# The samples' outer product in HGRN2 and retention heads: on VectorE with values broadcast by DMA, in place of row-tiled matmuls on TensorE

## The chip, the cores and the metric

The kernel runs on one core of a Trainium2 chip. The metric is the device time of one execution in microseconds. The profile is of one more execution of the same program, taken by the hardware profiler; all times inside it are counted from the start of its span.

## What is computed

Two decoder layers run on a prompt of 512 tokens and on 8 samples of one token each, which share the weights. Every layer has 16 heads of width 128: 4 of the HGRN2 kind, 6 of the mLSTM kind and 6 of the retention kind. Each sample brings a state of 128x128 for every head, takes one step and gives the new state back. For one token the HGRN2 and retention steps come to the same form: the state is scaled (by row in HGRN2, by one number in retention), the outer product of the token's key and value is added, and the query reads the result:

```
s_new = decay * s + k[:, None] * v[None, :]     # 8 samples, each head, 128 x 128
o     = q @ s_new
```

The reference has it as chunked scans whose chunk is one token long for the samples:

```python
s_new = (jnp.exp(b_last[:, :, 0, :])[..., None] * s
         + jnp.einsum('bhsk,bhsv->bhkv', kc * jnp.exp(b_last - b), vc))        # HGRN2
...
s_new = (chunk_d[None, :, None, None] * s
         + jnp.einsum('bhsk,bhsv->bhkv', kc * state_d[None, :, :, None], vc))  # retention
```

## The kernel before

**Tiles.** Activations lie transposed, features on partitions, with the 512 prompt tokens and the 8 sample tokens side by side as 520 columns (`TOK`; `T` is 512, `NS` is 8). A product of 128 output features with all tokens is one *tile*: 16 blocks of 128 inputs, each as three matmuls of 260 columns for two halves of the tokens (`quarter`), 96 matmuls in all, accumulated in the PSUM tensor `pj`. Weights come from HBM as 1 MB loads into `raw`; ScalarE makes their rounded part `whi`, GpSimd the rest `wlo`.

**Heads.** A head has four tiles, numbered 0 to 3: two for query and key (or the gate), one for v, one for the output gate z. The order of heads in a layer is one retention head, four HGRN2 heads, six mLSTM heads, five retention heads (`KINDS`). Head h of layer l has the number g = 16 l + h; n counts heads of one kind.

**The order of the work.** Each engine runs its own program in order, and the programs meet in semaphores. TensorE runs tile after tile. A tile is cut into eight *parts* of 12 matmuls, and between parts the small products of the heads are called (`hooks_of`): for retention and mLSTM heads `scores` and `rows` after part 1 of tile 3, `states_u` after part 4, `outputs` after part 7 (the tile's end); HGRN2 heads have `rows` after part 2, `states_u` after part 4, `outputs` after part 7. Layer 0's first head has `states_u` and `outputs` after parts 2 and 4 of the next head's tile 0. The z tile of the head is tile 3, the one in which all this stands.

**The samples' step in a plain head** (HGRN2 or retention) of before:
- ScalarE copies v (columns of all tokens) out of PSUM (`take(2, v, 0)`), then rounds the weights of a later tile (`high`), then copies the sample columns of q, k and v into `apart`, two to each group of 32 columns (`rows`, `by_four`).
- TensorE transposes v and k in chunks (`v_rows`, `k_rows`) and the three parts of `apart` (`sample_rows`), all into the PSUM tensor `mx`.
- ScalarE copies the samples' rows to `sr`, v's rows to `vt` and k's rows to `kt`. `vt` lies over the buffer `v`.
- VectorE spreads the samples' v over `big` in a block pattern (`blocks`), scales the state `ss` by the decay, and waits for `states_u`.
- TensorE, in `states_u`, forms the prompt's state increments from `kt` and `vt` (four products of 128x128), and in four row groups of two rows the samples' outer products from `sr` and `big` into columns 256 to 511 of `mx`.
- VectorE runs the chain of prompt states over four chunks into `st`, then adds the samples' products to `ss`. `outputs` on TensorE reads `st` and `ss`.

SyncE issues all DMAs of before in program order: weight loads (`load(t, par, src)`, which waits for the semaphore `lo_done` of the tile two before), the store of the last head's new states, the fetch of the next head's states (which waits until every earlier store has landed), and for mLSTM heads three rows broadcast from HBM. `big` is part of `lev`, a buffer that HGRN2 heads use for their levels.

## Time and profile before

| | us |
|---|---|
| median of 3 runs (2323.57 to 2324.18) | 2323.64 |
| profiled execution: its own time | 2323.17 |
| profiled execution: its span | 2321.6 |

| engine | busy us | share of the span |
|---|---|---|
| TensorE (matmul) | 2266.9 | 98% |
| VectorE | 1283.8 | 55% |
| GpSimd | 907.0 | 39% |
| ScalarE | 738.1 | 32% |

How to read the rows further down: PE is TensorE's matmul stream, PEld its weight loads, DVE is VectorE, ACT ScalarE, POOL GpSimd, SP or SPq SyncE's queue. L1046 is line 1046 of the kernel before. Matmuls overlap in the array, so the duration of one is longer than its distance from the next. A plain fp32 matmul is recorded as two. The profiler's timeline merges neighbours of one line and operands into one row with a count; its duration runs from the first start to the last end.

### The profile page before, as it was taken

How to read it: one execution, taken by the hardware profiler on the slowest of the kernel's cores; microseconds unless marked ns; L12 is line 12 of the kernel's file. 1: busy time of each engine (PE TensorE's matmuls, PEld its weight loads, DVE VectorE, ACT ScalarE, POOL GpSimd, SP SyncE). 2: the span in 40 equal slices, each digit the busy share in tenths (PEclk: the TensorE clock that was granted, in tenths of full speed). 3: DMA queues.
4: the chain of work that ended last, by engine and by line, in shares of the span. 5: the costliest groups of instructions: out<-in, count | busy, mean ns of one | idle time of the engine just before them, and what ended most of it. 6: DMA issues, size and time to landing. Idle time of an engine off the chain costs nothing.

```text
span 2321.6 us, 50275 instructions
## 1 busy us (share of the span) xinstructions
PE 2266.9 (98%) x21347; PEld 2161.7 (93%) x21347; DVE 1283.8 (55%) x2506; ACT 738.1 (32%) x1175; POOL 907.0 (39%) x668
## 2 busy tenths in 40 slices
PE   4899999999999999999999999999999999999998
PEld 3799999999999999998879999999999999999998
DVE  6346666677776344442126566567777753435444
ACT  2143322333333333421124333233333433334111
POOL 3033333333334343554333333333333443346542
PEclk9999999999999999999999999999999999999999
DMA  9952222554453333366775222244453333323332
GB/s 400 378 185 93 93 94 97 162 164 160 159 178 99 116 99 117 103 219 239 267 268 201 77 93 93 91 161 156 166 164 107 112 101 124 113 86 109 121 112 106
DMA packets 153647, 347.21 MB, mean 150 GB/s; under 512 B 14816, under 2 KB 85408, under 8 KB 127544
## 3 DMA queue, kind: packets, MB, share of 16 engines
q1 hardware_dynamic: 153424, 344.01, 43.1%
q8 instruction: 168, 2.75, 0.5%
q14 instruction: 55, 0.45, 0.1%
HBM read 312.07 MB, written 32.09 MB: 148 GB/s over the span
## 4 chain that ended last, share of the span: by engine, by line
PE 89%; DVE 4%; DMA 2%; DVEq 1%; POOL 1%; ACT 1%; issue 1%; SPq 0%; ACTq 0%; POOLq 0%
PE pj L685 72%; PE mx L691 3%; PE mx L1028 2%; DMA rows<-in_ada_first 1%; PE mx L1054 1%; PE mx L1042 1%; PE mx L778 1%; PE mx L744 1%; POOL wlo L653 1%; DMA spare_piece<-in_ada_first 1%; DVE t L1501 1%; PE pj L1150 1%; PE mx L1006 1%; PE mx L1056 1%; PE mx L1046 1%; PE mx L937 1%
## 5 line engine op out<-in xcount | busy, mean ns | idle before, releaser
L685 PE MATMUL pj<-hh,whi 128*128 128x260 f32 x4928 | 1418.0, 288 | 4.7 <-DVE hl L1501 3.2
L685 PE MATMUL pj<-hl,whi 128*128 128x260 f32 x4928 | 1392.8, 283 | 0.0
L685 PE MATMUL pj<-hh,wlo 128*128 128x260 f32 x4928 | 1390.6, 282 | 0.0
L653 POOL TENSOR_TENSOR wlo<-raw,whi 128x512 fp32r<-128x512 f32 x632 | 862.6, 1395 | 1323.5 <-ACT whi L1229 1323.5
L685 PEld LDWEIGHTS pj<-hh,whi 128*128 128x128 f32 x4928 | 928.1, 188 | 52.5 <-issue 46.2
L685 PEld LDWEIGHTS pj<-hl,whi 128*128 128x128 f32 x4928 | 928.5, 188 | 0.0
L685 PEld LDWEIGHTS pj<-hh,wlo 128*128 128x128 f32 x4928 | 928.0, 188 | 0.0
L1229 ACT ACTIVATE whi<-raw 128x2048 fp32r<-128x2048 f32 x158 | 302.9, 1917 | 256.8 <-PE pj L685 186.8
L1229 ACT ACTIVATE xv<-pj 128x260 f32<-128x260 f32 x188 | 64.7, 383 | 380.2 <-PE pj L685 379.9
L1501 DVE SCALAR_TENSOR_TENSOR o<-pj,mod,t 128x260 f32<-128x260 f32 (+1 forms) x56 | 24.6, 480 | 230.1 <-PE pj L685 214.5
L1229 ACT ACTIVATE t<-t 128x520 f32<-128x520 f32 (+1 forms) x126 | 79.2, 629 | 182.1 <-DVEq L1761 132.8
L1501 DVE SCALAR_TENSOR_TENSOR t<-xv,prm_bia,t 128x512 f32<-128x512 f32 x96 | 100.3, 1065 | 5.5
L1229 ACT ACTIVATE z<-pj 128x260 f32<-128x260 f32 x64 | 21.3, 385 | 242.0 <-PE pj L685 240.1
L1495 DVE TENSOR_TENSOR xv<-xv,lev 128x520 f32<-128x520 f32 x24 | 19.7, 819 | 121.7 <-ACT t L1229 121.2
L1495 DVE TENSOR_TENSOR t<-mx,hc 128x512 f32<-128x512 f32 x12 | 8.3, 692 | 112.0 <-PE mx L1006 112.0
L1229 ACT ACTIVATE zw<-zw 128x520 f32<-128x520 f32 x96 | 61.4, 639 | 25.0 <-DVEq L1734 20.7
L1495 DVE TENSOR_TENSOR zw<-zw,z 128x520 f32<-128x520 f32 x42 | 55.7, 1327 | 3.1
L724 PE MATMUL mx<-rows,sct 128*32 128x128 f32 x704 | 26.9, 302 | 30.7 <-DMA rows<-in_ada_first 30.6
L1495 DVE TENSOR_TENSOR lev<-sr,cst 98x256 f32<-98x256 f32 x44 | 36.8, 836 | 33.6 <-ACT sr L1229 33.6
L724 PEld LDWEIGHTS mx<-rows,sct 128*32 128x32 f32 x704 | 20.7, 121 | 35.2 <-issue 22.7
L691 PE MATMUL mx<-cst,xv 128*128 128x128 f32 x352 | 49.1, 273 | 1.6 <-DVEq L1991 1.5
L1951 DVE COPY xv<-mx 128x512 f32<-128x512 f32 x20 | 13.9, 693 | 65.4 <-PE mx L1065 65.4
(290 smaller groups left out, 2283.3 us busy)
## 6 DMA issues: line engine op xcount, KB each, us to landing
raw<-in_w_tiles SPq DMA_DIRECT2D x128, 1024.0 KB, 4.9
raw<-in_wo_tiles SPq DMA_DIRECT2D x32, 1024.0 KB, 5.0
lev<-in_w_ada SPq DMA_DIRECT2D x90, 256.0 KB, 4.6
rows<-in_ada_first SPq DMA_DIRECT2D x22, 1024.0 KB, 21.1
lev<-in_w_ada SPq DMA_DIRECT2D x39, 512.0 KB, 5.7
out<-ss SPq DMA_DIRECT2D x32, 512.0 KB
xv<-in_w_ada SPq DMA_DIRECT2D x25, 512.0 KB, 5.8
y_kept<-o SPq DMA_DIRECT2D x2, 4160.0 KB, 17.9
```

The lines of the kernel that those rows point to most:

```text
L653: last = e.tensor_tensor((wlo_third if t == 2 else wlo[:, par, :])[:, cs], w[:, cs], high_of(t)[:, cs].bitcast(F32), ALU.subtract)
L685: last = e.matmul(pj[:, 2 * par + b, 0:HALF], w[:, par, kb * P:(kb + 1) * P], x[:, kb, b * HALF:(b + 1) * HALF], start=(kb == 0 and m == 0 ...
L691: return e.transpose(out, src, cst[0:n, C_ID:C_ID + n])
L724: last = e.matmul(mx[32 * j:32 * j + 32, 2 + which, 0:n], sct[:, FIRST_K * i + x, :], w[:, j], start=(i == 0 and x == 0), stop=(p == piece ...
L744: last = e.matmul(mx[32 * j:32 * j + 32, 3, x * P:(x + 1) * P], sct[:, SESSION_K * (session % 4) + i, :], at[:, j * P:(j + 1) * P], start= ...
L778: last = e.matmul(mx[r:r + 32, n % 2, :], sct[:, kb, :], ada_slot(piece)[:, j, :], start=(kb < 4), stop=(kb >= KB - 4))
L937: last = e.matmul(mx[32 * j:32 * j + 2 * H_ML, 0, 0:QUART], gw[:, kb, :], x[:, kb, j * QUART:(j + 1) * QUART].bitcast(F32), start=(kb == 0 ...
L1006: last = e.matmul(mx[:, 0, c * CH:(c + 1) * CH], k[:, c * CH:(c + 1) * CH], q[:, c * CH:(c + 1) * CH], start=True, stop=True)
L1028: last = e.matmul(mx[64 * b:64 * b + 64, bank, 64 * c:64 * c + 64], key[:, s0:s0 + 64], query, start=True, stop=True)
L1229: return e.activation(out, in_, func, **kw)
L1495: return e.tensor_tensor(out, a_, b_, op)
L1501: return e.scalar_tensor_tensor(out=out, in0=a_, scalar=s, in1=b_, op0=op0, op1=op1)
```

## The change

The change applies to the HGRN2 and retention heads; mLSTM heads keep their way.

- After the copy of v, ScalarE issues a DMA that stores the samples' columns of v (128 partitions x 8) into a DRAM tensor `v_kept` of 8 rows of 128 floats (`keep_v`). The store's pieces are single floats.
- SyncE waits for that store, for the previous head to be done and for the head's last score products, and then issues a DMA that reads `v_kept` (4 KB) into `big` on each of the 128 partitions. It stands ahead of the load of the weight tile `t + 5`.
- TensorE's `sample_rows` and the products with `big` are only issued for mLSTM heads. `states_u` of retention heads (but layer 0's first) moves from part 4 to part 3 of tile 3.
- ScalarE drops the copies of `apart` and `sr` in plain heads, and waits for the store to have landed before it writes `vt`, which lies over v.
- VectorE drops `blocks` and the addition from PSUM in plain heads. The new `outer` multiplies `big` by the key columns and adds the product to `ss`: ahead of the chain of prompt states in HGRN2 heads, behind it in retention heads.

```diff
...
+        v_kept = nc.dram_tensor("v_kept", [NS, HD], F32, kind="Internal").ap()
...
+        v_saved, v_in = sem("v_saved"), sem("v_in")
...
+        def plain_before(g):
+
+            return sum(KINDS[x % NH] != "ml" for x in range(g))
...
                     for j in range(2):
                         if (l, h, j) == (0, 0, 0):
                             continue
+                        if j == 1 and kind != "ml":
+                            e.wait_ge(v_saved, 16 * (plain_before(g) + 1))
+                            e.wait_ge(head_done, g + 1)
+                            e.wait_ge(ps["score"], scorec(l, h, LEVELS + 1 if kind == "hg" else 1))
+                            e.dma_start(big, v_kept.rearrange("s d -> (s d)").partition_broadcast(P)).then_inc(v_in, 16)
...
                             v_rows()
-                            k_rows()
-                            sample_rows().then_inc(ps["tr"], 1)
+                            last = k_rows()
+                            if kind == "ml":
+                                last = sample_rows()
+                            last.then_inc(ps["tr"], 1)
...
                             e.wait_ge(vs["a"], g + 1)
-                            e.wait_ge(vs["blk"], g + 1)
                             e.wait_ge(as_["vt"], g + 1)
                             e.wait_ge(as_["kt"], g + 1)
-                            e.wait_ge(as_["sr"], g + 1)
+                            if kind == "ml":
+                                e.wait_ge(vs["blk"], n + 1)
+                                e.wait_ge(as_["sr"], n + 1)
                             w = HD + 1 if kind == "ml" else HD
                             for c in range(NC):
                                 last = e.matmul(mx[:, c, 0:w], kt[:, c, :], vt[:, c, 0:w], start=True, stop=True)
-                            lhs = sw if kind == "ml" else sr[:, 1, :]
-                            for j in range(4):
-                                r = slice(32 * j, 32 * j + 2)
-                                last = e.matmul(mx[:, j, 256:512], lhs[r, :], big[r, 0:256], start=True, stop=True)
+                            if kind == "ml":
+                                for j in range(4):
+                                    r = slice(32 * j, 32 * j + 2)
+                                    last = e.matmul(mx[:, j, 256:512], sw[r, :], big[r, 0:256], start=True, stop=True)
...
-                        return ({}, {}, {1: (scores, rows), 4: (states_u,), 7: (outputs,)}), {5: (back,)}
+                        return ({}, {}, {1: (scores, rows), 3: (states_u,), 7: (outputs,)}), {5: (back,)}
...
                             last.then_inc(taken, 1)
+                            if kept is not None:
+                                kept()
...
                         def rows(scaled):
...
+                            e.wait_ge(ps["tr"], g + 1)
+                            if scaled == "ml":
+                                act(sr[0:GR], mx[0:GR, 3, 0:3 * HD].rearrange("p (j d) -> p j d", j=3), ACT.Copy).then_inc(as_["sr"], 1)
                             else:
...
+                                e.wait_ge(v_saved, 16 * (plain_before(g) + 1))
                             act(vt[:, :, 0:HD], mx[:, 1, :].rearrange("p (c d) -> p c d", c=NC), ACT.Copy).then_inc(as_["vt"], 1)
...
+                        def keep_v():
+
+                            e.wait_ge(taken, ht(g, 2))
+                            e.wait_ge(v_in, 16 * plain_before(g))
+                            e.dma_start(v_kept.rearrange("s d -> d s"), v[:, T:TOK],
+                                        allow_slow_non_contiguous=True).then_inc(v_saved, 16)
...
-                            take(2, v, 0)
+                            take(2, v, 0, kept=keep_v)
...
-                        else:
-                            blocks(sr[0:GR, 2, :], big[0:GR, 0:256])
-                        e.drain().then_inc(vs["blk"], 1)
+                            e.drain().then_inc(vs["blk"], 1)
...
+                        def outer():
+
+                            e.wait_ge(v_in, 16 * (plain_before(g) + 1))
+                            vb = big.rearrange("p (s d) -> p s d", s=NS)
+                            tt(vb, vb, bc(k[:, T:TOK], 2, HD), M)
+                            e.drain()
+                            tt(ss, ss, vb, A_)
+                            e.drain()
+
+                        if kind == "hg":
+                            outer()
                         e.wait_ge(ps["u"], g + 1)
...
-                        tt(ss4, ss4, mx[:, 0:4, 256:512], A_)
+                        if kind == "ml":
+                            tt(ss4, ss4, mx[:, 0:4, 256:512], A_)
+                        elif kind == "rt":
+                            outer()
                         e.drain().then_inc(vs["ss"], 1)
```

What stands in a row on the engines is shown at three places. Line numbers are those of each kernel; the words in brackets are the semaphores that an instruction waits for.

ScalarE, retention head 12 of layer 0, from the copy of v to the copy of z; `xv` holds the buffers of v and `vt`, `t` that of `kt`. Before:

```order
L1229 ACTIVATE xv<-pj 128x260 [waits tile_done]
L1229 ACTIVATE xv<-pj 128x260
L1229 ACTIVATE whi<-raw 128x2048 [waits tile_done,raw_in0]
L1229 ACTIVATE apart<-xv 128x12x2 [waits taken,v_qk,p_tr,hc_in0]
L1229 ACTIVATE sr<-mx 98x384 [waits p_tr]
L1229 ACTIVATE xv<-mx 128x4x128
L1229 ACTIVATE t<-mx,hc 128x512
L1229 ACTIVATE z<-pj 128x260 [waits tile_done,head_done]
```

The same place now:

```order
L1244 ACTIVATE xv<-pj 128x260 [waits tile_done]
L1244 ACTIVATE xv<-pj 128x260
L1408 DMA v_kept<-xv 128x8x1 [waits v_in,taken]
L1244 ACTIVATE whi<-raw 128x2048 [waits tile_done,raw_in0]
L1244 ACTIVATE xv<-mx 128x4x128 [waits v_saved,p_tr,hc_in0]
L1244 ACTIVATE t<-mx,hc 128x512
L1244 ACTIVATE z<-pj 128x260 [waits tile_done,head_done]
```

The copies to `apart` and `sr` are gone, the store stands right behind the copy of v, and the copy to `vt` waits for it.

VectorE, HGRN2 head 2 of layer 0, from the last score level to the copy of the outputs; `lev` holds `big`. Before:

```order
L1865 COPY t<-mx 64x4x64
L1495 TENSOR_TENSOR lev<-sr,cst 98x256 [waits a_sr]
L1495 TENSOR_TENSOR ss<-ss,t 128x1024 [waits state_in1]
L1906 COPY st<-mx 128x128 [waits stored,p_u]
L1501 SCALAR_TENSOR_TENSOR st<-st,sm,mx 128x128 x3
L1495 TENSOR_TENSOR ss<-ss,mx 128x1024
L1951 COPY xv<-mx 128x512 [waits p_o]
```

The same place now:

```order
L1886 COPY t<-mx 64x4x64
L1516 TENSOR_TENSOR ss<-ss,t 128x1024 [waits state_in1]
L1516 TENSOR_TENSOR lev<-lev,xv 128x1024 [waits v_in]
L1516 TENSOR_TENSOR ss<-ss,lev 128x1024
L1937 COPY st<-mx 128x128 [waits stored,p_u]
L1522 SCALAR_TENSOR_TENSOR st<-st,sm,mx 128x128 x3
L1985 COPY xv<-mx 128x512 [waits p_o]
```

Product and sum moved ahead of the chain and wait for the broadcast; the addition behind the chain is gone.

SyncE, from the loads during retention head 11 of layer 0 to the fetch for head 13; `lev` holds `big`. Before:

```order
L403 DMA raw<-in_w_tiles 128x2048 [waits lo_done] x4
L478 DMA out<-ss 128x8x128 [waits v_ss]
L487 DMA out<-st 128x128 [waits v_chain]
L458 DMA ss<-in_state_ret 128x8x128 [waits head_done,stored]
L464 DMA hc<-in_hc 128x653
```

The same place now:

```order
L409 DMA raw<-in_w_tiles 128x2048 [waits lo_done]
L557 DMA lev<-v_kept 128x1024 [waits p_score,head_done,v_saved]
L409 DMA raw<-in_w_tiles 128x2048 [waits lo_done] x3
L484 DMA out<-ss 128x8x128 [waits v_ss]
L493 DMA out<-st 128x128 [waits v_chain]
L464 DMA ss<-in_state_ret 128x8x128 [waits head_done,stored]
```

The broadcast stands ahead of three weight loads and of the store of the head's states.

## Rows read from the trace of the kernel before

**Rows 1.** The page: engines' busy time, instructions; then the chain's shares by engine
```profile
PE 2266.9 (98%) x21347; PEld 2161.7 (93%) x21347; DVE 1283.8 (55%) x2506; ACT 738.1 (32%) x1175; POOL 907.0 (39%) x668
...
PE 89%; DVE 4%; DMA 2%; DVEq 1%; POOL 1%; ACT 1%; issue 1%; SPq 0%; ACTq 0%; POOLq 0%
```

**Rows 2.** TensorE's groups by form: count, then busy us, mean ns, idle before
```profile
L691 PE MATMUL mx<-cst,apart 128*98 128x128 f32 x96 | 15.8, 273 | 0.0
...
L1046 PE MATMUL mx<-lev,sr 2*128 2x256 f32 x160 | 14.3, 426 | 0.0
```

**Rows 3.** Timeline, TensorE, retention head 12, layer 0: start us, duration us, line, operands
```profile
814.59 0.49 PE L691 MATMUL mx<-cst,apart 128*98 128x128 f32 x3
814.84 0.37 PE L685 MATMUL pj<-hh,whi 128*128 128x260 f32 x1
...
819.24 1.06 PE L1042 MATMUL mx<-xv,t 128*128 128x128 f32 x8
820.23 0.71 PE L1046 MATMUL mx<-lev,sr 2*128 2x256 f32 x8
820.87 0.39 PE L685 MATMUL pj<-hh,whi 128*128 128x260 f32 x1
```

**Rows 4.** Timeline, ScalarE, the same head: copies of v, sr, vt, kt; whi
```profile
810.16 0.67 ACT L1229 ACTIVATE xv<-pj 128x260 f32<-128x260 f32 x2 [7.17 <-PE pj L685]
...
815.12 0.49 ACT L1229 ACTIVATE sr<-mx 98x384 f32<-98x384 f32 x1 [2.38 <-PE mx L691]
815.51 0.59 ACT L1229 ACTIVATE xv<-mx 128x512 f32<-128x512 f32 x1
815.99 0.69 ACT L1229 ACTIVATE t<-mx,hc 128x512 f32<-128x512 f32 x1
...
826.12 1.91 ACT L1229 ACTIVATE whi<-raw 128x2048 fp32r<-128x2048 f32 x1
```

**Rows 5.** DMA issues by operands: count, KB each, median us from issue to landing
```profile
raw<-in_w_tiles SPq DMA_DIRECT2D x128, 1024.0 KB, 4.9
...
ss<-in_state_ret SPq DMA_DIRECT2D x12, 512.0 KB, 4.1
...
t<-in_c_cols SPq DMA_DIRECT2D x1, 72.0 KB, 2.0
```

**Rows 6.** Timeline, VectorE, head 12: the chain's start, the samples' addition behind it
```profile
821.01 0.29 DVE L1906 COPY st<-mx 128x128 f32<-128x128 f32 x1 [2.03 <-PE mx L1046]
...
822.75 1.22 DVE L1495 TENSOR_TENSOR ss<-ss,mx 128x1024 f32<-128x1024 f32 x1 [0.17 <-issue]
```

**Rows 7.** Timeline, HGRN2 head 2, layer 0: ScalarE's copy of v, TensorE's outputs
```profile
246.32 0.67 ACT L1229 ACTIVATE xv<-pj 128x260 f32<-128x260 f32 x2 [13.54 <-PE pj L685]
...
262.20 0.61 PE L1054 MATMUL mx<-xv,t 128*128 128x128 f32 x4
```

**Rows 8.** Timeline, SyncE: layer 0's last mLSTM head, then a retention head
```profile
727.26 0.33 SPq L403 DMA_DIRECT2D raw<-in_w_tiles  x1
727.63 0.43 SPq L476 DMA_DIRECT2D out<-cvk  x1
...
728.59 1.09 SPq L482 DMA_DIRECT2D out<-nr  x2
729.72 0.44 SPq L483 DMA_DIRECT2D out<-st  x1
...
740.91 0.39 SPq L458 DMA_DIRECT2D ss<-in_state_ret  x1
...
780.60 0.33 SPq L403 DMA_DIRECT2D raw<-in_w_tiles  x1
...
788.21 0.39 SPq L458 DMA_DIRECT2D ss<-in_state_ret  x1
```

**Rows 9.** Windows: stretch, us, busy of each engine (instructions), granted clock, DMA, GB/s
```profile
1217.00:1220.30 3.30, 1.43 (x16) 1.01 (x9) 2.89 (x7) 0.97 (x2) 0.00 (x0) 1.00 0.62 189
1220.30:1223.70 3.40, 3.40 (x16) 1.50 (x16) 2.55 (x4) 0.75 (x2) 0.00 (x0) 0.50 0.01 2
```

More of the change, by code:

```diff
@@ L970, in sample_rows @@
                             e.wait_ge(vs["qk"], g + 1)
-                            e.wait_ge(as_["apart"], g + 1)
+                            e.wait_ge(as_["apart"], n + 1)
                             for j, at in enumerate((1, 2, 0)):
@@ L983, in k_rows @@
                             for c in range(NC):
-                                tr(mx[:, 2, c * HD:(c + 1) * HD], kw[:, c * CH:(c + 1) * CH], P)
+                                last = tr(mx[:, 2, c * HD:(c + 1) * HD], kw[:, c * CH:(c + 1) * CH], P)
+                            return last
                         def rows():
@@ L1341, in head, with take @@
                         hc = hc2[:, g % 2]
-                        def take(j, dst, off, scale=1.0, swapped=None):
+                        def take(j, dst, off, scale=1.0, swapped=None, kept=None):
                             t = t0 + j
@@ L1366, in rows @@
                         def rows(scaled):
-                            if g:
-                                e.wait_ge(ps["tr"], g)
-                            e.wait_ge(taken, ht(g, 2))
-                            vqk = xv[:, 2 * (PAD + TOK):2 * (PAD + TOK) + 3 * TOK].rearrange("p (m t) -> p m t", m=3)[:, :, T:TOK]
-                            if scaled == "hg":
-                                act(by_four(apart[:, 1:2, :]), by_four(x1[:, PAD + T:PAD + TOK].unsqueeze(1)), ACT.Copy)
-                                last = act(by_four(apart[:, 0:3:2, :]), by_four(vqk[:, 0:3:2, :]), ACT.Copy)
-                            else:
-                                e.wait_ge(vs["qk"], g + 1)
-                                last = act(by_four(apart[:]), by_four(vqk), ACT.Copy)
-                            last.then_inc(as_["apart"], 1)
-                            e.wait_ge(ps["tr"], g + 1)
-                            act(sr[0:GR], mx[0:GR, 3, 0:3 * HD].rearrange("p (j d) -> p j d", j=3), ACT.Copy).then_inc(as_["sr"], 1)
+                            if scaled == "ml":
+                                e.wait_ge(taken, ht(g, 2))
+                                vqk = xv[:, 2 * (PAD + TOK):2 * (PAD + TOK) + 3 * TOK].rearrange("p (m t) -> p m t", m=3)[:, :, T:TOK]
+                                e.wait_ge(vs["qk"], g + 1)
+                                act(by_four(apart[:]), by_four(vqk), ACT.Copy).then_inc(as_["apart"], 1)
+                            e.wait_ge(ps["tr"], g + 1)
+                            if scaled == "ml":
+                                act(sr[0:GR], mx[0:GR, 3, 0:3 * HD].rearrange("p (j d) -> p j d", j=3), ACT.Copy).then_inc(as_["sr"], 1)
+                            else:
+                                e.wait_ge(v_saved, 16 * (plain_before(g) + 1))
                             act(vt[:, :, 0:HD], mx[:, 1, :].rearrange("p (c d) -> p c d", c=NC), ACT.Copy).then_inc(as_["vt"], 1)
@@ L1388, in rows @@
                             last.then_inc(as_["kt"], 1)
+                        def keep_v():
+                            e.wait_ge(taken, ht(g, 2))
+                            e.wait_ge(v_in, 16 * plain_before(g))
+                            e.dma_start(v_kept.rearrange("s d -> d s"), v[:, T:TOK],
+                                        allow_slow_non_contiguous=True).then_inc(v_saved, 16)
                         def log1p_exp(dst, src):
@@ L1442, in head @@
                             take(1, x1, PAD, SCALE)
-                            take(2, v, 0)
+                            take(2, v, 0, kept=keep_v)
                             rows("hg")
@@ L1882, in low_first @@
                                 tt(hl[:, kb, :], o[:, kb, :], hh[:, kb, :].bitcast(F32), S_).then_inc(o_lo_first, 1)
-                        e.wait_ge(as_["sr"], g + 1)
                         if kind == "ml":
+                            e.wait_ge(as_["sr"], n + 1)
                             ts(sw[0:GR], sr[0:GR, 2, :], gs[0:GR, i, 1:2], None, M)
```

## The prediction

> **What bounds the kernel now.** I read the page's busy shares first, then the chain of work that ended last: TensorE is busy 98% of the span and 89% of the chain is its own [rows 1]. Another engine or a transfer costs time only where TensorE has to wait for it, and what TensorE no longer issues is saved one for one. So the question for each edit is what it takes off TensorE's queue and whether TensorE then waits. TensorE takes its instructions in order: a wait at `states_u` or `outputs` holds up the tile behind it.
>
> **What the change takes off TensorE.** In each of the 20 heads that are not mLSTM it drops three transposes of sample columns and the four-way product of `big` (eight recorded matmuls). The groups by form show 96 transposes for all 32 heads and 160 product matmuls for the 20 [rows 2]. Their mean durations, 273 and 426 ns, are no prices, because matmuls overlap; the price is the distance to the next instruction in the timeline. In head 12 of layer 0 (retention) the three transposes hold the engine from 814.59 to 814.84 and the product from 820.23 to 820.87 [rows 3]: 0.25 + 0.64 = 0.89 us a head, 17.8 us in all.
>
> **What it adds on TensorE's path.** Three steps follow one another from the moment ScalarE has copied v, and each is waited for.
>
> First, ScalarE stores the samples' v to `v_kept`, 1024 pieces of 4 bytes, and may not write `vt` over v before that store has landed. Call the time from the end of the copy of v to that landing S. In head 12 v is copied at 810.16 + 0.67 = 810.83; `vt` and `kt` take from 815.51 to 815.99 + 0.69, that is 1.17 [rows 4]. With 0.3 us for three semaphores, an estimate, `states_u` cannot start before 812.3 + S. It now stands 24 tile matmuls behind the transposes instead of 36. In before 36 took 814.84 to 819.24, 4.40 us, so 24 take 2.93 and TensorE is there at 814.59 + 2.93 = 817.5. **It waits S - 5.2 us.** Before, nothing of a transfer stood there.
>
> Second, SyncE waits for the store and fetches `v_kept` into all partitions, 512 KB. A state of the same size lands after 4.1 us [rows 5]; I take that. Third, VectorE multiplies and adds, two operations of 128x1024, each as long as the addition it drops, 1.22 us, and a chain of 1.74 us (821.01 to 822.75) lies before it or behind [rows 6].
>
> In a retention head the chain runs first. `outputs` is 48 tile matmuls (5.87 us) after `states_u` ends, and chain, product, sum and 0.4 for semaphores take 4.6, so this hides with 1.3 us to spare. The fetch would have landed by then too: 810.8 + S + 4.3 is before the chain's end for every S up to 5.2, and with a larger S `states_u` moves along with it. In an HGRN2 head product and sum come ahead of the chain. v is copied at 246.99 [rows 7], so `ss` and `st` are ready at 246.99 + S + 4.1 + 2.44 + 1.74 + 0.6 (semaphores and drains, estimate) = 255.9 + S, and `outputs`, now at 262.20 less 0.25 and 0.64, wants them at 261.3: **it waits S - 5.4 us.**
>
> Layer 0's first head has `outputs` only 24 matmuls (2.93 us) after `states_u`, while chain, product and sum take 4.7 with semaphores: a stall of 1.8, less 0.89, is +0.9 whatever S is.
>
> **The price of S.** No engine but SyncE issues a DMA in before, and nothing in it stores 1024 small pieces, so I bound it. From below: a plain 72 KB transfer lands after 2.0 us, one of 1024 pieces of 512 bytes after 4.1 [rows 5]. The nearest row by kind is the one store of before that scatters 4-byte pieces, the normalizer `st` of line 483 in the 12 mLSTM heads: 128 pieces that fill one row of 512 bytes. Its landing shows where SyncE fetches the next state, since that waits for every store before it [rows 8]. In a retention head the fetch comes 788.21 - 780.60 = 7.6 us after the 1 MB load that stands ahead of the stores; in the last mLSTM head of layer 0 it comes 740.91 - 727.26 = 13.65 us after that load. The difference, 6.0 us, has four more stores behind it: 11 KB in pieces of 88 bytes, twice 2 KB in pieces of 512, and the 128 pieces of 4 bytes. I put it on the last, for pieces of 512 bytes are what the retention head stores too, 1152 of them, without that time. `v_kept` is eight such rows. If they drain side by side, S is 2.0 + 6.0 = 8.0 to 4.1 + 6.0 = 10.1; in two lots, 2.0 + 12.0 = 14.0; one after another, 2.0 + 48 = 50. If 4 bytes cost nothing special, it is 2.0 to 4.1. I take 9.0: the piece count alone is not the price (1024 pieces land after 4.1), and the row of the same kind has the 6.0.
>
> The Trainium skill ("DMA: Bandwidth & Descriptors", section "Anatomy of one DMA") speaks the other way: a DMA costs about 2.0 us and its bytes over 436 GB/s, so by its formula, which was fitted on the GpSimd path, 4 KB are 2.0 us and the sum would be the first rival's. The same page's "Rules for kernel authors" says that a strided last dimension lowers to one descriptor per element and should be rearranged, which names this store; it gives no price.
>
> **The clock.** Where TensorE had little to do at 1217.0 to 1220.3 (busy 1.43 of 3.30 us, clock 1.00), the next 3.4 us show a granted clock of 0.50, the lower level of 1.2 GHz [rows 9]: 1.7 us of work lost. A stall of 3.8 us leaves the engine idle longer than that stretch did. I charge 1.7 us to each of the 11 later retention heads; in HGRN2 heads the wait is split between `states_u` and `outputs`, and I charge nothing.
>
> **The sum, with S = 9.0.** 11 retention heads: 3.8 - 0.89 = 2.9 each, 32 us. 8 HGRN2 heads: 3.6 - 0.89 = 2.7 each, 22 us. First head 0.9. Clock 11 x 1.7 = 19. Together +73 us on the profiled execution's 2323.2 us, 2396 (the median of the runs shown is 0.5 us higher, which is ignored).
>
> **What lies beside.** ScalarE issues the store (SyncE's issues take 0.4 us [rows 8]) and drops the copies of `apart` and `sr`; it idles 2.38 us ahead of them in before [rows 4]. SyncE's load of the tile after next now stands behind the wait for the store: with S = 9.0 it is issued near 820.4 and lands 4.9 us later [rows 5], behind 512 KB more, by 827; ScalarE wants it at 826.12 [rows 4] plus the stall of 3.8 less 0.89, 829. The cover is thin but whole, and it grows with S. VectorE's work grows by about 0.8 us a head (two operations of 1.22 for one and a smaller one), all in the stretches reckoned above. mLSTM heads keep their instructions. The 1 MB load that would share the DMA engines with the store is itself held back by SyncE's wait.
>
> **Rivals.**
> 1. *4-byte pieces are cheap.* S below 5.2, the store hides behind the score matmuls and two parts of a tile: 19 x 0.89 saved less 0.9 = -16 us, 2307. Place: ScalarE's wait before `vt`. It decides at S = 6.1, where stall and saving are equal. For it: the plain transfers of 72 KB and 512 KB land after 2.0 and 4.1 us [rows 5]. Against it: the 6.0 us behind line 483.
> 2. *Eight rows drain one after another.* S = 50: 43.9 x 11 + 43.7 x 8 + 0.9 + clock 19 x 1.7 = +866 us, 3189. For it: 128 pieces already cost 6.0, and the number of pieces is eightfold. Against it: eight separate rows, and nothing shows two of them waiting for one another.
> 3. *Between the first rival and the forecast*, S from 5.2 to 7.5: 2307 to 2345, crossing zero.
> 4. *Between the forecast and the second rival*, S of 14 to 40.
> That the change does not do what it says can be left out: the order of instructions shows transposes and product gone and nothing else new on TensorE.
>
> **How the numbers follow.** Forecast (S from 8 to 14) 0.55: from 2359 (S = 8.0, no clock loss: 1.9 x 11 + 1.7 x 8 + 0.9 = 35) to 2505 (S = 14.0, clock lost in all 19 heads: 7.9 x 11 + 7.7 x 8 + 0.9 + 32 = 182). Cheap pieces 0.20. Between them 0.07. S of 14 to 40: 0.08. One after another 0.10. The range leaves the last two out: 2304 to 2505. Within 0.2% (4.6 us, about what a measurement here tells from no change) is a slice of the third case, 0.04; faster is the first rival and a rest of the third, 0.22; slower 0.74.
>
> **What would show it.** In the profile of the changed kernel the DMA list gives issue to landing for `v_kept<-xv`: 8 to 14 us by the forecast, under 5 by the first rival. ScalarE's idle time before `xv<-mx` (`vt`) should be released by that DMA, and TensorE should idle before `states_u` in retention heads by S - 5.2 and before `states_u` and `outputs` in HGRN2 heads by S - 5.4 together. The granted clock should show dips behind the longer stalls. The fetch `lev<-v_kept` should land after about 4 us; 10 or more would move the wait to `outputs` in every head and make the forecast too low. If TensorE shows no such idle time, the first rival holds.

## The result, and the profile after

The changed kernel takes 2423.51 us, the median of four runs (2419.05 to 2428.00), against 2323.91 for the kernel before beside it: a ratio of 1.0425, 95% interval 1.0412 to 1.0438. It is slower by 99.6 us, where the prediction said 73. The profiled execution took 2425.28 us, with a span of 2423.5 us (before 2321.6) and a mean granted clock of 0.979 (before 0.997).

The page first, as [rows 1] was read: busy time of the engines, then the shares of the chain that ended last, by engine and by line.

```profile
PE 2285.8 (94%) x21127; PEld 2182.1 (90%) x21127; DVE 1281.6 (53%) x2506; ACT 730.4 (30%) x1127; POOL 924.8 (38%) x668
...
PE 77%; DMA 12%; DVE 4%; POOL 2%; ACT 2%; issue 1%; DVEq 1%; SPq 0%; ACTq 0%
PE pj L696 63%; DMA v_kept<-xv 7%; DMA lev<-v_kept 2%; PE mx L702 2%; DMA rows<-in_ada_first 1%; PE mx L1069 1%; PE mx L1042 1%; PE mx L789 1%; POOL wlo L664 1%; PE mx L755 1%; PE mx L1057 1%; POOL hl L669 1%; DVE t L1522 1%; PE pj L1165 1%; PE mx L1071 1%
```

TensorE's share of the chain fell from 89% to 77%, and 9% now lies on the two new transfers. What TensorE waits for, between 116 and 2421 us (line, releaser: us in all, times, longest):

```profile
PE mx L1057 <- ACT t L1244: 56.5, 20, 4.4
PE mx L1069 <- DVEq L1948: 23.4, 10, 3.4
PE pj L696 <- POOL wlo L664: 4.3, 6, 1.4
```

Line 1057 is `states_u`, line 1069 `outputs`. In the kernel before neither stands in this view. Behind the releaser of the first, ScalarE's copies of `vt` and `kt`, stands the store, and VectorE's product stands behind the broadcast (the same view for ScalarE and for VectorE):

```profile
ACT xv L1244 <- DMA v_kept<-xv: 145.6, 20, 15.3
...
DVE lev L1516 <- DMA lev<-v_kept: 80.3, 19, 9.8
```

Head 12 of layer 0, the head of [rows 3, 4, 6], in the timeline (start, duration, engine, line, operands, idle time before and releaser): ScalarE with its store, SyncE, TensorE, VectorE.

```profile
843.83 0.67 ACT L1244 ACTIVATE xv<-pj 128x260 f32<-128x260 f32 x2 [7.17 <-PE pj L696]
844.52 0.37 ACTq L1408 DMA_DIRECT2D v_kept<-xv  x1
...
853.56 0.60 ACT L1244 ACTIVATE xv<-mx 128x512 f32<-128x512 f32 x1 [6.65 <-DMA v_kept<-xv]
854.05 0.68 ACT L1244 ACTIVATE t<-mx,hc 128x512 f32<-128x512 f32 x1
```

```profile
853.47 0.33 SPq L557 DMA_DIRECT2D lev<-v_kept  x1
```

```profile
851.02 0.28 PE L696 MATMUL pj<-hl,whi 128*128 128x260 f32 x1
854.88 1.28 PE L1057 MATMUL mx<-xv,t 128*128 128x128 f32 x8 [3.58 <-ACT t L1244]
```

```profile
856.20 0.29 DVE L1937 COPY st<-mx 128x128 f32<-128x128 f32 x1 [5.61 <-PE mx L1057]
...
859.15 1.22 DVE L1516 TENSOR_TENSOR lev<-lev,xv 128x1024 f32<-128x1024 f32 x1 [1.39 <-DMA lev<-v_kept]
860.45 1.23 DVE L1516 TENSOR_TENSOR ss<-ss,lev 128x1024 f32<-128x1024 f32 x1
```

The store leaves at 844.52. Two engines wait for it and both go on together, SyncE at 853.47 and ScalarE at 853.56: S, the time from the copy of v to the landing of the store, is 9.0 us, as forecast, and 9.05 is the median over the 20 heads by the same reading (8.2 to 10.1, but 17.6 in the first head). By the page the queue of these 20 stores moved 20800 packets, 1040 for each store of 1024 pieces. TensorE, done with its tile at 851.3, starts `states_u` at 854.88, 3.6 us later.

An HGRN2 head, head 2 of [rows 7], pays twice: TensorE before `states_u` and before `outputs`, and VectorE in between, where product and sum stand ahead of the chain.

```profile
273.11 1.13 PE L1057 MATMUL mx<-xv,t 128*128 128x128 f32 x8 [2.46 <-ACT t L1244]
280.69 0.71 PE L1069 MATMUL mx<-xv,t 128*128 128x128 f32 x4 [2.11 <-DVEq L1948]
```

```profile
276.21 1.23 DVE L1516 TENSOR_TENSOR lev<-lev,xv 128x1024 f32<-128x1024 f32 x1 [9.68 <-DMA lev<-v_kept]
277.52 1.23 DVE L1516 TENSOR_TENSOR ss<-ss,lev 128x1024 f32<-128x1024 f32 x1
278.89 0.29 DVE L1937 COPY st<-mx 128x128 f32<-128x128 f32 x1
```

The broadcast (DMA issues: count, KB, median us to landing) took 5.3 us and not the 4.1 of [rows 5]:

```profile
lev<-v_kept SPq DMA_DIRECT2D x20, 512.0 KB, 5.3
```

Last the clock behind the wait of head 12, to be set against [rows 9] (stretch, length, busy us and instructions of PE, PEld, DVE, ACT, POOL, granted clock, DMA share, GB/s). The engine idles for most of 3.1 us, and the next 3.4 us are granted at the lower level, 1.2 GHz. Twenty such stretches, of 3.4 or 6.8 us, lie between 100 and 2230 us, 88.7 us in all. Seventeen of them begin in or right behind the waits of a plain head: in all 11 later retention heads, and in six of the eight HGRN2 heads. The first two HGRN2 heads of layer 0, head 2 above among them, show none, though they wait as long.

```profile
852.60:855.70 3.10, 0.82 (x7) 0.85 (x8) 0.00 (x0) 1.17 (x2) 0.34 (x1) 1.00 0.14 13
855.70:859.10 3.40, 3.40 (x18) 3.40 (x18) 1.34 (x4) 0.00 (x0) 0.00 (x0) 0.50 0.95 260
859.10:862.50 3.40, 3.40 (x30) 3.40 (x30) 2.45 (x2) 0.00 (x0) 0.00 (x0) 1.00 1.00 424
```

Where the 102 us of span went can be read head by head, from the start of `outputs` in the two timelines. "Waits" are the gaps between the starts of TensorE's matmuls ahead of `states_u` and `outputs`, less the usual 0.12 us (a little more than the idle time of 79.9 above), "saved" is 1.17 us a head (an experiment below shows where that comes from), and the rest is the measured delay less the waits, plus what was saved.

| heads | waits | saved | measured delay | rest |
|---|---|---|---|---|
| the first | 5.5 | 1.2 | 6.1 | 1.8 |
| 11 other retention heads | 41.0 | 12.9 | 51.9 | 23.8 |
| 8 HGRN2 heads | 38.2 | 9.4 | 41.1 | 12.3 |
| 12 mLSTM heads | 0 | 0 | 3.3 | 3.3 |
| all | 84.7 | 23.4 | 102.4 | 41.2 |

The clock can account for most of the rest. In time lost at the lower clock, 2423.5 x 0.021 - 2321.6 x 0.003 = 43.9 us were added; that is an upper bound, since TensorE idles in part of those stretches. Of the 12.3 us in HGRN2 heads, 4.8 lie in head 1 alone, where TensorE also sat idle for 2.4 us at line 948, the projection of the gates (0.3 in the kernel before), for a reason that the profile does not show.

### The profile page after: what moved, and what is told of

Read it like the earlier page. It is cut to its first block, busy times and chain, and to the rows that moved or that the text cites. A ratio compares the mean times of both kernels' runs of the same rounds, so it can differ in the third digit from the quotient of the medians.

```text
span 2423.5 us, 49836 instructions
## 1 busy us (share of the span) xinstructions
PE 2285.8 (94%) x21127; PEld 2182.1 (90%) x21127; DVE 1281.6 (53%) x2506; ACT 730.4 (30%) x1127; POOL 924.8 (38%) x668
## 3 DMA queue, kind: packets, MB, share of 16 engines
q10 hardware_dynamic: 20800, 0.08, 0.4%
## 4 chain that ended last, share of the span: by engine, by line
PE 77%; DMA 12%; DVE 4%; POOL 2%; ACT 2%; issue 1%; DVEq 1%; SPq 0%; ACTq 0%
PE pj L696 63%; DMA v_kept<-xv 7%; DMA lev<-v_kept 2%; PE mx L702 2%; DMA rows<-in_ada_first 1%; PE mx L1069 1%; PE mx L1042 1%; PE mx L789 1%; POOL wlo L664 1%; PE mx L755 1%; PE mx L1057 1%; POOL hl L669 1%; DVE t L1522 1%; PE pj L1165 1%; PE mx L1071 1%
## 5 line engine op out<-in xcount | busy, mean ns | idle before, releaser
L664 POOL TENSOR_TENSOR wlo<-raw,whi 128x512 fp32r<-128x512 f32 x632 | 877.7, 1419 | 1402.2 <-ACT whi L1244 1402.2
L696 PEld LDWEIGHTS pj<-hh,whi 128*128 128x128 f32 x4928 | 938.4, 190 | 51.6 <-issue 41.2
L696 PEld LDWEIGHTS pj<-hl,whi 128*128 128x128 f32 x4928 | 937.9, 190 | 0.0
L696 PEld LDWEIGHTS pj<-hh,wlo 128*128 128x128 f32 x4928 | 937.8, 190 | 0.0
L1057 PE MATMUL mx<-xv,t 128*128 128x128 f32 (+1 forms) x256 | 43.9, 326 | 56.5 <-ACT t L1244 56.5
L1057 PEld LDWEIGHTS mx<-xv,t 128*128 128x128 f32 x256 | 38.5, 230 | 60.0 <-issue 60.0
L1069 PE MATMUL mx<-xv,t 128*128 128x128 f32 (+1 forms) x256 | 47.5, 289 | 23.4 <-DVEq L1948 23.4
L1516 DVE TENSOR_TENSOR lev<-lev,xv 128x1024 f32<-128x1024 f32 x20 | 26.0, 1299 | 80.5 <-DMA lev<-v_kept 80.3
L1244 ACT ACTIVATE xv<-mx 128x512 f32<-128x512 f32 (+1 forms) x36 | 20.4, 573 | 151.1 <-DMA v_kept<-xv 145.6
L1069 PEld LDWEIGHTS mx<-xv,t 128*128 128x128 f32 x256 | 38.2, 200 | 25.5 <-DVEq L1948 25.5
```

The source lines that it names most:

```text
L664: last = e.tensor_tensor((wlo_third if t == 2 else wlo[:, par, :])[:, cs], w[:, cs], high_of(t)[:, cs].bitcast(F32), ALU.subtract)
L696: last = e.matmul(pj[:, 2 * par + b, 0:HALF], w[:, par, kb * P:(kb + 1) * P], x[:, kb, b * HALF:(b + 1) * HALF], start=(kb == 0 and m == 0 ...
L1057: last = e.matmul(mx[:, c, 0:w], kt[:, c, :], vt[:, c, 0:w], start=True, stop=True)
L1069: last = e.matmul(out, a[:, c, :], vt[:, c, 0:w], start=True, stop=(c == 0))
L1244: return e.activation(out, in_, func, **kw)
L1516: return e.tensor_tensor(out, a_, b_, op)
```

## The experiments

Two theories stood at the start. **The pieces**: S is 9 us because the store writes 1024 neighbouring 4-byte pieces, and everything else (waits, clock) follows from S. **Its place**: the time lies in ScalarE's new wait ahead of `vt`, in the broadcast of 512 KB or in VectorE's longer row of operations, whatever the pieces are. Within the first, what matters could be the number of pieces or that they are neighbours.

**Stores alone.** The kernel before, with extra stores of constant columns on ScalarE's queue in place of the change; nothing waits for them but the end of the program. The shapes in short:

```diff
+ whole: to.rearrange("s d -> d s") <- cst[:, 0:8]       # as the change does it
+ one, two, four: the same with 1, 2, 4 columns
+ apart, alone: 1024 pieces, 16 and 64 bytes from one another
+ wide: to[128, 8] <- cst[:, 0:8]                        # 128 pieces of 32 bytes
```

> The kernel before, with stores of a constant from ScalarE's queue into scratch DRAM at quiet places, one shape for each name, nothing waiting for them before the end. Theory (pieces of 4 bytes that neighbour each other in a row of 512 bytes are taken in one at a time, rows side by side): one row of 128 pieces (one1) lands after 7 to 9 us, and two, four and eight rows (two2, four4, whole8) hardly later, 8 to 10 us; with pieces 16 bytes apart (apart4) 3 to 5 us, 64 bytes apart (alone16) 2 to 4 us, though both have the 1024 pieces of whole8; 128 pieces of 32 bytes (wide32) 2 to 3 us. Rival (the price is by the number of pieces): one1 2 to 3 us, two2 3, four4 5, whole8 9, apart4 and alone16 9 as well, wide32 2 to 3.

The kernel took 2323.41 us in one run beside 2323.69 for before, so the stores cost nothing as such. Their landings (DMA issues: count, KB each, median us to landing; the list has none for `four`):

```profile
apart<-cst ACTq DMA_DIRECT2D x5, 4.0 KB, 4.2
whole<-cst ACTq DMA_DIRECT2D x5, 4.0 KB, 12.1
wide<-cst ACTq DMA_DIRECT2D x4, 4.0 KB, 2.7
...
alone<-cst ACTq DMA_DIRECT2D x3, 4.0 KB, 3.7
one<-cst ACTq DMA_DIRECT2D x3, 0.5 KB, 8.6
two<-cst ACTq DMA_DIRECT2D x2, 1.0 KB, 10.2
```

This settles what makes S long. Three of the rows have 1024 pieces of 4 bytes: 12.1 us where they touch, 4.2 and 3.7 where they lie 16 or 64 bytes apart. One row of 128 touching pieces already takes 8.6, and eight rows add only 3.5 to it: the touching pieces of a row are the price, the rows drain mostly side by side, and the number of pieces matters little. `two` and `whole` came out above the 8 to 10 us that I expected, and `whole` 3 us above S in the changed kernel. Each of the five `whole` stores had a 1 MB weight load in flight beside it for part of its time, while in the changed kernel SyncE issues no load until the store has landed; whether that is the reason was not tested.

**The change with 32-byte pieces.** One edit: `v_kept` is laid out as it lies in `v`, and VectorE reads the broadcast with a step of 32 bytes instead.

```diff
- v_kept = nc.dram_tensor("v_kept", [NS, HD], ...)
+ v_kept = nc.dram_tensor("v_kept", [HD, NS], ...)
...
- e.dma_start(big, v_kept.rearrange("s d -> (s d)").partition_broadcast(P))...
+ e.dma_start(big, v_kept.rearrange("d s -> (d s)").partition_broadcast(P))...
...
- e.dma_start(v_kept.rearrange("s d -> d s"), v[:, T:TOK],
-             allow_slow_non_contiguous=True).then_inc(v_saved, 16)
+ e.dma_start(v_kept, v[:, T:TOK]).then_inc(v_saved, 16)
...
- vb = big.rearrange("p (s d) -> p s d", s=NS)
+ vb = big.rearrange("p (d s) -> p s d", s=NS)
```

> The changed kernel with v_kept laid out as 128 rows of 8 samples, so that the store has 128 pieces of 32 bytes; the broadcast is the same 4 KB, and VectorE reads it with a stride of 8. Theory (the 4-byte pieces make the store long): the landing falls from 9 us to 2 to 4, the waits before states_u and outputs go except in layer 0's first head, the clock stays up, and the time is 2303 to 2315 us, below the kernel before. Rival (storing to HBM and reading back takes this long whatever the pieces): landing 7 to 9 us, 2400 to 2430 us.

2328.13 us, ratio 1.0017 (1.0008 to 1.0027): 95 of the 99.6 us are gone with this edit alone, and the waits before `states_u` with them. The store now lands after 1.4 us (median). The gain over the kernel before that I expected, 2303 to 2315 us, did not come. What TensorE still waits for, and VectorE in a retention head:

```profile
PE mx L1069 <- DVEq L1947: 19.5, 17, 4.2
```

```profile
823.31 2.22 DVE L1515 TENSOR_TENSOR lev<-lev,xv 128x1024 f32<-128x1024 f32 x1 [0.17 <-issue]
825.61 2.18 DVE L1515 TENSOR_TENSOR ss<-ss,lev 128x1024 f32<-128x1024 f32 x1
```

With a step in their operand the two operations take 2.2 us each instead of 1.22 (up to 3.1 where GpSimd works beside them), and `outputs` waits 0.8 us for them in a retention head (0.3 to 0.6 in HGRN2, 3.8 in each layer's last head, 4.3 in the first). So nearly all the saving is spent again, now in VectorE. The second theory keeps only this remainder.

**ScalarE's wait away.** The samples' v are copied to a tile of their own, `v8`, and stored from there, so that `vt` need not wait for the store.

```diff
+ act(v8[:], v[:, T:TOK], ACT.Copy)...
...
+ e.dma_start(v_kept.rearrange("s d -> d s"), v8[:], ...)      # instead of from v
...
- e.wait_ge(v_saved, 16 * (plain_before(g) + 1))               # ahead of vt
```

> The changed kernel with the samples' columns of v copied to a buffer of their own, from which the 4-byte pieces are stored, so that ScalarE writes vt without waiting for the store. Theory (the store is late for everything behind it, and the broadcast that follows it is due next): the wait moves from states_u to outputs, about 4 us in retention heads as before and 5 us in HGRN2 heads, and the time stays within 15 us of the changed kernel, 2405 to 2430 us. Rival (the wait that guards vt is what costs): its 57 us and the clock loss of the retention heads go, 2340 to 2370 us.

2453.65 us, ratio 1.0557 (1.0540 to 1.0575), worse than the change by 30 us. Some 10 us of that go with S, which has a median of 9.85 us in this run: two more runs of the change, with S at 9.84 and 9.90, took 2433.61 and 2436.78 us (below), so at the same S this kernel is worse by 17 to 20 us. The wait is not gone, it stands whole before `outputs`:

```profile
PE mx L1070 <- DVEq L1949: 111.6, 20, 7.6
```

The place of the wait is therefore not the cause. My own expectation, within 15 us of the change, was missed as well: there are 5 us of wait in a retention head (6 in each layer's last) and 6 to 7 in an HGRN2 head, where the change splits its wait in two and `states_u` is done in between, and the stretches at half clock grow with them (mean clock 0.971).

**TensorE kept busy.** The changed kernel with matmuls ahead of `states_u` whose results nobody reads: 32 in a retention head, 16 in an HGRN2 head; then the retention heads alone, beside the unaltered change on the same chip.

```diff
+ if kind == "rt" and g:                    # first run: also "hg", with 16
+     e.wait_ge(head_done, g + 1)
+     for _ in range(32):
+         e.matmul(mx[:, 3, 0:256], hh[:, KB - 1, 0:P], hh[:, KB - 1, 0:256], start=True, stop=True)
```

> The changed kernel with extra matmuls whose result nobody reads, put ahead of the wait at states_u: 32 of 256 columns in retention heads (3.4 us), 16 in HGRN2 heads (1.7 us). All waits stay as late as they were. Theory (a part of the loss is TensorE at its lower clock after each wait): the granted clock stays at the upper level in retention heads and the time falls by 20 to 40 us although TensorE does more, 2383 to 2404 us. Rival (the clock has no share, the whole loss is waiting): no faster than the changed kernel, 2418 to 2432 us.

> The changed kernel unaltered, on the chip of this call, as the measure for the runs beside it. Every theory: 2419 to 2430 us, waits before states_u and outputs 80 us in all, half-clock stretches 85 us in all.

> The changed kernel with 32 matmuls of 256 columns, whose results nobody reads, ahead of states_u in the retention heads alone, so that TensorE works while it waits for the samples' values; the HGRN2 heads are as in the change. Theory (beyond the waits of 80 us, the change loses about 40 us to the half clock behind them, 1.2 to 2.4 us in each retention head): the clock loss of the 11 heads goes, some 15 us, against filler that runs past the end of the wait by up to 1 us a head: 2405 to 2415 us where the change gives 2424 on the same chip, and the half-clock stretches fall by 40 us or more. Rival (the half clock costs nothing that counts, the waits alone do it): within 3 us of the change or above it, though the half-clock stretches fall.

The first run gave 2426.20 us, ratio 1.0441 (1.0425 to 1.0456): no gain, with HGRN2 heads that were later than in the change, and with no run of the change beside it (S was 9.75 us here). It settles nothing by itself. In the other two the change took 2433.61 us (ratio 1.0472, 1.0457 to 1.0486), with S at a median of 9.84 us on that chip, and the filled one 2423.63 (1.0432, 1.0416 to 1.0448) with S at 9.85: 10.0 us less, for more work. 58 us from the wait of head 29 (a retention head of layer 1) on, the filled kernel first, then the change, in the columns of the windows above:

```profile
2090.00:2148.00 58.00, 57.49 (x484) 56.54 (x483) 20.52 (x39) 17.65 (x29) 22.18 (x17) 1.00 0.34 108
```

```profile
2100.40:2158.40 58.00, 53.89 (x435) 53.15 (x435) 20.91 (x39) 17.64 (x28) 21.63 (x16) 0.94 0.35 108
```

With the wait filled the clock stays at 1.00, and heads 28 to 30 lose 3.6 to 3.8 us each instead of 5.3 to 5.4. So the half clock behind these waits costs at least 1.6 us a head on top of the wait, for in these heads the filling and what was left to wait took about 0.4 us longer than the wait alone (4.6 to 4.8 against 4.2 to 4.4). Over all 11 heads the gain is 1.2 us a head in the mean. It was less than I expected of the whole kernel (10 us, not 15).

**A version that keeps the saving.** The 32-byte pieces, a buffer of its own for the broadcast (so that it need not wait for the scores), a product that reads with a step but writes whole rows, and product and sum ahead of the chain everywhere, in the last head also ahead of the residual halves.

```diff
+ vbig = sb("vbig", P, NS * HD)
+ apart = vbig[:, 0:384].rearrange("p (j d) -> p j d", j=3)
...
- e.wait_ge(ps["score"], ...)
- e.dma_start(big, v_kept...)
+ e.dma_start(vbig[:], v_kept.rearrange("d s -> (d s)").partition_broadcast(P))...
...
- tt(vb, vb, bc(k[:, T:TOK], 2, HD), M)
+ tt(vb, vbig[:].rearrange("p (d s) -> p s d", s=NS), bc(k[:, T:TOK], 2, HD), M)
...
- if kind == "hg":
+ if kind != "ml":
      outer()
...
```

> The change with its store in whole 32-byte pieces (v_kept as 128 rows of 8 samples), a buffer of its own for the broadcast, so that it no longer waits for the scores, the product written sample by sample so that the sum runs on whole rows, and product and sum ahead of the chain in the retention heads too and ahead of the residual halves in the last head. Theory (the 4-byte pieces cost 95 of the 99.6 us, and what was left in the run with 32-byte pieces, 19.5 us of waits before outputs, is the strided product and sum and the late broadcast): the waits go but for some 4 us in the first head, the 0.89 us per plain head stay saved: 2308 to 2314 us, ratio 0.993 to 0.996, clock as before. Rival (the broadcast of 512 KB and VectorE's product are themselves on the path wherever they stand): outputs still wait 0.5 to 1 us in each plain head, 2322 to 2330 us.

2309.34 us, ratio 0.9941 (0.9929 to 0.9954): faster than both kernels, than the kernel before by 0.6%. Waits; the transfers; VectorE in head 12, and GpSimd beside it:

```profile
PE mx L1069 <- DVEq L1944: 7.4, 3, 3.0
```

```profile
vbig<-v_kept SPq DMA_DIRECT2D x20, 512.0 KB, 4.4
v_kept<-xv ACTq DMA_DIRECT2D x20, 4.0 KB, 1.4
```

```profile
811.43 2.96 DVE L1515 TENSOR_TENSOR lev<-vbig,xv 128x1024 f32<-128x1024 f32 x1
814.47 2.09 DVE L1515 TENSOR_TENSOR ss<-ss,lev 128x1024 f32<-128x1024 f32 x1
```

```profile
807.75 7.73 POOL L664 TENSOR_TENSOR wlo<-raw,whi 128x512 fp32r<-128x512 f32 x4 [5.18 <-ACT whi L1244]
```

S is 1.4 us at the median, but 11.1 in the first head, and three waits are left, in the first head and in the last of each layer. The other plain heads gain 1.17 us each on before, with few exceptions, and not 0.89. The rest of the difference lies beside what was dropped; the same head's transposes of v and k and its `states_u` in this kernel, each with the matmul behind it, then the start of the transposes in the kernel before:

```profile
808.19 1.04 PE L702 MATMUL mx<-cst,xv 128*128 128x128 f32 x8
808.99 0.37 PE L696 MATMUL pj<-hh,whi 128*128 128x260 f32 x1
...
811.95 1.05 PE L1057 MATMUL mx<-xv,t 128*128 128x128 f32 x8
812.76 0.36 PE L696 MATMUL pj<-hh,whi 128*128 128x260 f32 x1
```

```profile
813.72 1.04 PE L691 MATMUL mx<-cst,xv 128*128 128x128 f32 x8
```

Here `states_u` holds TensorE 0.81 us to the next tile, where its eight matmuls took 820.23 - 819.24 = 0.99 ahead of the product [rows 3]. The transposes of v and k hold it 0.80 us, where they took 814.59 - 813.72 = 0.87 [rows 3].

**One kind of head at a time.** The same version, in which either the HGRN2 heads or the retention heads do as the change does.

```diff
+ v_rows = nc.dram_tensor("v_rows", [NS, HD], ...)
...
+ if kind == NARROW:        # "hg" in one run, "rt" in the other: store, broadcast and product as changed
```

> The version with 32-byte pieces and a buffer of its own (ratio 0.994 to before), in which the 8 HGRN2 heads alone do as the change does: store in 4-byte pieces, broadcast into the shared buffer. Theory A (as predicted: an HGRN2 head costs its waits, 5.2 us in the changed kernel and 6.2 on the chip of the second call, and no clock): 8 x 5.2 to 6.2 = 42 to 50 us more than that version, 2351 to 2359 us where before is 2324. Theory B (the half clock follows these waits too, 1.5 to 3 us a head): 54 to 74 us more, 2363 to 2383, with half-clock stretches of 30 us or more between 120 and 410 us and 1270 and 1600 us.

> The same the other way round: the 12 retention heads alone do as the change does, the HGRN2 heads have the 32-byte pieces. Theory (11 waits before states_u of 3.9 to 4.8 us, 1.5 us of clock behind each, and 5 to 6 us in the first head): 43 to 53 + 16 + 6 = 65 to 75 us more than the version with 32-byte pieces, 2374 to 2385 us where before is 2324. Without a loss by the clock it would be 49 to 59 us more. Rival (the heads of one kind disturb those of the other, by the queue of SyncE or the transfers): the two losses do not add up to the 114 to 124 us that lie between that version and the changed kernel.

> The changed kernel unaltered, as the measure on the chip of this call: 2419 to 2436 us, by S of 9.0 to 10.5 us there. The losses of the two runs beside it should add up to its distance from the version with 32-byte pieces.

HGRN2 alone took 2372.83 us (ratio 1.0213, 1.0198 to 1.0228), retention alone 2387.85 (1.0278, 1.0261 to 1.0295), the change 2436.78 (1.0487, 1.0470 to 1.0504). The version with 32-byte pieces would be 0.9941 x 2323.29 = 2309.6 on this chip, so the two kinds lose 63 and 78 us; I had expected 65 to 75 of the retention heads. Their waits, HGRN2 first:

```profile
PE mx L1075 <- DVEq L1956: 34.4, 11, 4.1
PE mx L1063 <- ACT t L1250: 14.4, 8, 2.3
```

```profile
PE mx L1063 <- ACT t L1250: 56.7, 12, 6.0
```

Three of the 11 waits before `outputs` in the first are those that the version has anyway (7.4 us there). In the HGRN2 heads themselves 43.6 us of waits became a delay of 59.4, and the stretches in question show the lower clock (80 to 420 us in the windows; the second is the version without the narrow store):

```profile
80.00:420.00 340.00, 307.60 (x3203) 289.45 (x3196) 176.36 (x430) 97.01 (x152) 108.18 (x76) 0.95 0.39 135
```

```profile
80.00:420.00 340.00, 330.81 (x3579) 315.19 (x3572) 213.83 (x461) 109.73 (x172) 127.51 (x86) 1.00 0.45 155
```

Theory B holds and the prediction's step falls: behind the waits of all eight HGRN2 heads the lower clock stands here, for 3.4 or 6.8 us, and they lose 59.4 - 43.6 = 15.8 us beyond their waits, or 2 us a head. The heads of the kind that was left alone moved by 0.03 us or less each, with three exceptions: 1.7 us in the head right behind the first with the retention heads changed, and 2.6 us in the first head and 0.3 in head 16 with the HGRN2 heads changed. So one kind hardly disturbs the other. Still the two losses make 141 us where the change loses 127. By the timelines 6 us of that excess lie in the retention heads, which waited 55 us in their own run and 52 in the change on that chip; the rest is spread, and why is open.

## Why the prediction was right, and where it was off

The direction, the place and the mechanism were right: slower, by TensorE's waits for the store of `v_kept`, priced from the one 4-byte store of before. The time lay in the range, 27.5 us above the forecast. Step by step:

- **Saved on TensorE**, 0.89 us a head: too small. It is 1.17 us, since the operations beside the dropped product get shorter too. 20 heads save 23.4, not 17.8.
- **S = 9.0**: right, 9.05 by the median, but that it fits so closely is partly luck. It was picked from 8.0 to 14.0, the same store alone took 12.1 us, and two more runs of the change had 9.84 and 9.90. The piece count is not the price, as argued. The reason given, that a row's touching pieces cost and eight rows drain side by side, is what the stores alone show: 8.6 us for one row, 12.1 for eight, 4 for as many pieces that don't touch. The rival of cheap pieces fell with them, as did the one of rows in series. By the formula of the Trainium skill ("DMA: Bandwidth & Descriptors", section "Anatomy of one DMA"), which the page fitted on the GpSimd path, these 4 KB would land after an estimated 2.0 us. The 32-byte pieces come near that (1.4 us in two kernels, 2.7 among the stores alone), the touching 4-byte pieces do not.
- **Retention heads wait S - 5.2 = 3.8**: right, 41.0 / 11 = 3.7 us, and `outputs` hides its chain, product and sum but for 0.4 us in one head. The 0.3 us put in for semaphores came out at 0.24: in head 12, 854.88 - 853.47 = 1.41 us from SyncE's start to `states_u`, of which ScalarE's two copies take 1.17.
- **HGRN2 heads wait 3.6**: mis-sized, 38.2 / 8 = 4.8 us. The working was right and two terms were not: store and broadcast together took 9.4 + 5.1 = 14.5 us in the mean of these heads, where 9.0 + 4.1 = 13.1 was put in. The broadcast is not slow as such, for with 32-byte pieces it lands after 4.3 us. In each of these heads the changed kernel issues two weight loads of 1 MB within 0.9 us behind it, the kernel with 32-byte pieces one. That may be the reason; no run tests it, and in the first head, where both kernels issue two, the broadcast took 4.5 and 4.2 us.
- **The first head loses 0.9 whatever S is**: wrong. `outputs` waits 1.9 us as forecast, but `states_u` waits 3.6 before it, for S is 17.6 in this head. I took the S of a later head for one that I had not looked at. The pieces are not all of it: with 32-byte pieces S is still 11.5 us in this head (11.1 in the last version). In the changed kernel a store of 4160 KB, `y_kept<-o`, is under way there until 16 us behind the issue; whether that is the reason was not tested.
- **The clock, 1.7 us in the 11 retention heads and nothing in HGRN2**: the price was near where it was tested (at least 1.6 us in three heads, 1.2 in the mean of the 11), its reach was not. A wait that is split between two places still brought the lower clock, in six of eight HGRN2 heads here and in all eight in the run with HGRN2 heads alone, 2 us a head there. In the retention heads the rest is 23.8 us against 19 charged. How much of that is clock is not settled: other waits grew by a few us too (3 us for `wlo` over all heads).
- **What was costed at nothing** held: mLSTM heads show no new waits (their 3.3 us stand behind heads 4 and 20 and belong to the clock), and the load behind SyncE's wait came nearly in time: ScalarE's waits for the tiles' weights grew from 15.9 to 23.8 us, and TensorE's waits for `wlo` by the 3 us above.

By the same terms the sum is 28 us (retention) + 29 (HGRN2) + 4 (first head) + 41 (clock, and small waits) = 102, against 32 + 22 + 0.9 + 19. Of the 28 us missing, 22 are the last term. Among the rivals, the third ends at 2349 us by the prediction's own terms (S = 7.5), not at 2345; nothing hangs on it.

What was not foreseen as a way out: the change itself, without its 4-byte pieces, with a buffer of its own and with product and sum moved ahead, is worth 14 to 15 us.

## What to carry to other kernels

Before a value is sent through HBM to be broadcast, look at how its pieces touch: lay the destination out so that each partition writes one run, and do the transposition where it is read. A wait of 4 us on TensorE cost more than 4 us here where the clock fell behind it, so charge the clock for each such wait, split or not, as a cost that comes in most heads and not in all. When an operation is dropped, price it with its neighbours, and look at the first head by itself.

## What the runs showed of the hardware

- 1024 pieces of 4 bytes into HBM land after 12.1 us where they touch and after 3.7 to 4.2 where they lie 16 or 64 bytes apart; 128 touching ones take 8.6.
- A VectorE operation of 128x1024 takes 1.22 us alone and 2.09 with GpSimd at work beside it (the sums in the changed kernel and in the last version, above); with a step of 32 bytes in place it takes 2.22 alone. The product of the last version, which reads with that step and writes whole rows, took 2.10 alone in the first head and 2.96 beside GpSimd in the head shown, but 2.17 to 2.29 in five HGRN2 heads, with GpSimd at work as well. In the changed kernel both operations ran at 1.22 or 1.23 in 18 of 20 heads, where GpSimd was idle. The addition that the change drops reads PSUM and took 1.22 us in either case (three times with GpSimd at work). The Trainium skill ("SBUF — State Buffer", section "SBUF: two separate sides") says that a VectorE operation with two SBUF inputs and a GpSimd one that reads SBUF exclude one another. The longer times with SBUF inputs and the unchanged one with PSUM agree with that; how the wait falls in each case no row here separates.
- S for the same kernel differed by chip or run, 9.05, 9.84 and 9.90 us at the median, and the time went with it: 2423.5, 2433.6 and 2436.8 us.
